# The shared expert's last gate and up quarter, moved ahead of the first pair's row picking

## The reference, cut to what matters

```
scores = sigmoid(xf @ router_w)                     # 256 tokens x 64 experts
idx    = top_k(scores + router_b, 6)
wts    = sel / sum(sel) * 2.5
routed = sum over a token's 6 experts of ((silu(x @ w_gate[e]) * (x @ w_up[e])) @ w_down[e]) * weight
shared = (silu(xf @ sh_gate) * (xf @ sh_up)) @ sh_down
x = x + g2 * (routed + shared)
```

## Time and profile before

| what | us |
|---|---|
| median of 3 runs | 1473.63 |
| lowest and highest of them | 1473.15, 1475.94 |
| the profiled execution's own time | 1474.18 |
| its span, first to last instruction | 1472.3 |
| PE busy | 1311.8 (89%) |
| DVE busy | 631.6 (43%) |
| ACT busy | 296.9 (20%) |
| HBM read | 496.57 MB, 340 GB/s over the span |

### The profile page before, as it was taken

The page is one execution under the profiler, slowest core; times in us unless marked ns, Lnnn a source line. Parts: engine busy times, 40 slices in busy tenths (PEclk is TensorE's granted clock), DMA queues, the critical chain, the costliest instruction groups (busy, mean ns, idle before and its releaser), DMA issues.

```text
span 1472.3 us, 21785 instructions
## 1 busy us (share of the span) xinstructions
PE 1311.8 (89%) x9040; PEld 684.9 (47%) x9040; DVE 631.6 (43%) x1165; ACT 296.9 (20%) x504; POOL 66.7 (5%) x116
## 2 busy tenths in 40 slices
PE   4998868999999879888898999989999978888888
PEld 1444325764444334344346766875444433333334
DVE  5997733254433222232234688654443222232232
ACT  3236322321111111111112113031111111111110
POOL 0000681000000000000000000000000000000000
PEclk9999889999999999999997999999999999999999
DMA  9672972958999999999999772575899999999996
GB/s 379 251 179 75 175 283 92 397 226 341 400 422 421 429 423 428 428 430 426 429 419 324 289 256 94 233 323 223 355 422 421 425 428 428 428 430 427 427 426 246
DMA packets 50583, 502.78 MB, mean 341 GB/s; under 512 B 9324, under 2 KB 16236, under 8 KB 19820
## 3 DMA queue, kind: packets, MB, share of 16 engines
q1 hardware_dynamic: 49932, 499.18, 85.1%
q10 hardware_dynamic: 544, 2.10, 0.3%
HBM read 496.57 MB, written 4.69 MB: 340 GB/s over the span
## 4 chain that ended last, share of the span: by engine, by line
PE 59%; DMA 32%; DVE 4%; issue 2%; ACT 1%; SPq 1%; DVEq 0%; ACTq 0%
PE ps L704 54%; DMA arena<-in_w_experts 28%; DMA arena<-in_ada_w 4%; PE ps L428 2%; PE ps L1011 2%; SPq L472 1%; ACT arena L1323 1%; DVE arena L1941 1%; PE ps L749 0%; DMA arena<-in_mcst 0%; DVE arena L1775 0%; DVE arena L1776 0%; PE ps L957 0%; DVE arena L1793 0%; DVE arena L1773 0%
## 5 line engine op out<-in xcount | busy, mean ns | idle before, releaser
L704 PE MATMUL ps<-arena 128*32 128x512 f32 (+13 forms) x8220 | 1227.0, 487 | 138.5 <-issue 52.3
L704 PEld LDWEIGHTS ps<-arena 128*32 128x32 f32 (+6 forms) x8220 | 622.9, 131 | 728.8 <-issue 589.7
L1323 ACT ACTIVATE arena<-ps 128x512 f32<-128x512 f32 (+7 forms) x304 | 168.0, 553 | 943.2 <-PE ps L704 799.2
L1982 DVE SCALAR_TENSOR_TENSOR arena<-arena,ps 128x256 f32<-128x256 f32 x44 | 21.2, 481 | 242.1 <-ACT arena L1323 242.1
L1323 ACT ACTIVATE arena<-arena 128x256 f32<-128x256 f32 (+7 forms) x140 | 91.6, 680 | 162.8 <-DVE arena L2002 58.6
L2000 DVE CAST arena<-ps 128x512 bf16<-128x512 f32 x42 | 29.1, 692 | 164.9 <-PE ps L704 164.9
L1937 DVE COPY arena<-ps 128x512 f32<-128x512 f32 x44 | 30.4, 692 | 135.5 <-PE ps L704 135.5
L1970 DVE TENSOR_TENSOR arena<-arena 128x1024 bf16<-128x1024 f32 x42 | 51.5, 1225 | 37.3 <-ACT arena L1323 37.0
L694 POOL MEMSET arena<- 128x1 f32 x2 | 0.2, 102 | 1206.1 <-PE ps L1011 1206.1
L1011 PE MATMUL ps<-arena 128*128 128x128 f32 x352 | 52.8, 273 | 0.0
L2002 DVE TENSOR_TENSOR arena<-ps,arena 128x1024 f32<-128x1024 f32 x42 | 51.4, 1224 | 1.8 <-DVE arena L2000 0.4
(11 more groups left out here) (226 smaller groups left out, 475.3 us busy)
## 6 DMA issues: line engine op xcount, KB each, us to landing
arena<-in_w_experts SPq DMA_DIRECT2D x76, 3072.0 KB, 20.8
arena<-in_w_experts SPq DMA_DIRECT2D x52, 2048.0 KB, 19.5
arena<-in_w_experts SPq DMA_DIRECT2D x52, 1024.0 KB, 18.9
arena<-in_ada_w SPq DMA_DIRECT2D x40, 1024.0 KB, 6.1
arena<-in_hy_w_in SPq DMA_DIRECT2D x6, 2048.0 KB, 11.2
arena<-in_ada_w SPq DMA_DIRECT2D x4, 2048.0 KB, 22.3
arena<-in_w_shared SPq DMA_DIRECT2D x2, 3072.0 KB, 10.5
arena<-in_hy_w_out SPq DMA_DIRECT2D x1, 4096.0 KB, 13.3
```

What stands on the lines that cost most here:

```text
L704: return pe.matmul(out, lhsT, rhs, start=start, stop=stop, skip_group_check=skip)
L1323: return act.activation(out, in_, func, **kw)
L1982: stt(hh, sg, wtab[:, n:n + 1], ps[:, GU, FF:2 * FF], M, M).then_inc(sem("h_done"), 1)
```

## The change

One line moves. The fourth quarter of the shared expert's gate and up product, with its `sh_gu`, is issued right behind the third one and ahead of `pick_rows(0)`, where it was behind `turn_rows(0)`.

```diff
                 mm(ps[0:1, 0, 3 * NE:4 * NE], extent, ident[:, 0:NE], True, True).then_inc(sem("route_mm"), 1)
                 shared_gate_up(2)
+                shared_gate_up(3).then_inc(sem("sh_gu"), 1)
                 pick_rows(0)
                 find_tokens(0)
                 turn_rows(0)
-                shared_gate_up(3).then_inc(sem("sh_gu"), 1)
```

## The result

The changed kernel is slower by a little. Its median is 1478.13 us (20 runs, 1471.74 to 1481.46) against 1474.10 us for the kernel before in the same comparison, a ratio of 1.0022 with a 95% interval of 1.0011 to 1.0032. That is +3.2 us (+1.6 to +4.7); the two medians themselves differ by 4.0. Forecast were 1475.4 us, or +1.76, which lies in the lower part of that interval.

A forecast was written before the change was run, and what follows sets the result against it. PE was taken to bound each layer's expert part until the loads' stage starts at 370, the loads after that. A new wait of 0.88 us per layer, 1.76 in all, on 1473.63 gave 1475.4 us, 8 in 10 within 1473.0 to 1478.5.

The forecast's parts named there:

- The bound: Each layer's expert part: PE's progress up to 370 sets when the loads begin, so its lost time reaches the layer's end.
- loads' stage: Second stage of each layer's expert part, from the triple issued at 370.0: loads run without a gap, at 422 GB/s.
- The quarter covers the copy: Behind the turning the quarter hid DVE's copy of the turned rows; moving it bares a wait, taken as 0.88 us per layer.
- The cover ahead of the picking is empty: Ahead of the picking PE never waited, so the quarter covers nothing there and picking and turning start 3.40 us later.
- The queues: Behind the turning: DVE's shared expert product starts near 324.5 with 4 us left; SP's earlier load gains nothing.
- load at place 5: SP's 2 MB load that waits for the quarter: issued 5.7 us earlier, near 315.8, worth nothing at 370.
- The clock: Around group 0's gate and up product: granted clock expected to stay up despite PE's pauses of 0.69 and 0.86 us.
- The whole: Whole kernel: 1475.4 us, which is 1473.63 + 1.76, or 0.12%; chance of the same within 0.2%: 0.80.
- +0.88 in layer 0, +0.88 again: Sum over both layers' expert parts: one new wait each, passed on undiminished, 1.76 us in all.
- forecast's own 1474 to 1477.5: Whole kernel: range with scatter of medians if only a wait of 0.7 to 1.2 us per layer is added; 76 in 100.
- 1473.0 to 1478.5 of 8 in 10: Whole kernel: wider range, reaching to the case of no move and to most of the falling clock's case.
- the clock's rival: Group 0's gate and up product: clock falls to 1.2 GHz, 2.57 us per layer with the wait, 1478.8; 9 in 100.

The follow-up runs named there:

- split kernels: Kernel before with the fourth quarter halved around the turning, in one version also two steps of quarter 1 moved ahead of the routing wait: ratios 0.9999, 0.9995, 0.9995.
- e4: Kernel before with the fourth quarter moved whole between the table look-up and the turning: ratio 1.0003 (0.9988 to 1.0018).
- f4: Kernel before with the third quarter too moved behind the turning, ahead of the fourth: ratio 1.0050 (1.0034 to 1.0067).
- f2: Kernel before with DVE's copy of the first pair's turned rows made four times per layer instead of once: ratio 1.0004 (0.9991 to 1.0017).
- f3: Changed kernel with DVE's copy of the first pair's turned rows made four times per layer: ratio 1.0081 (1.0055 to 1.0108).
- f1: Changed kernel, with the first half of the load at place 5 waiting for group 0's gate and up product: ratio 1.0023 (1.0008 to 1.0039).
- g1: Kernel before, unaltered, compared with itself as if it were a changed one: ratio 1.0006 (0.9992 to 1.0020).
- e1: Changed kernel run again with no edit, against the kernel before: ratio 1.0024 (1.0008 to 1.0040).
- split quarter: Kernel before with the fourth quarter halved, one half ahead of the turning, one behind it: ratios 0.9999 and 0.9995 in two comparisons.
- g2: Changed kernel a third time, no edit, on the same chip as the unaltered kernel before: ratio 1.0047 (1.0029 to 1.0065).

## Why the prediction was right, and where it was short

**The bound.** Right. PE sets the start of the loads' stage, and the distance shifts as PE does; the stage behind it gives nothing back. Between the triple's issue and the first load for the next layer's mixer lie 397.35 us before and 397.17 after, and from layer 1's triple to the first store of the output 412.69 and 412.76. (In layer 0 the split kernels have 397.8 to 398.3, but so have e4 and f4 with 397.8 and 397.9, so this is not laid to the split.)

**The quarter covers the copy.** Right, and shown by f2 and f3. Forecast 0.88 per layer, measured 0.95 and 0.94: 0.86 to 0.88 of it is the pause, and nearly all of the rest is that the quarter takes 3.46 us ahead of the picking and had filled 3.40 behind the turning. The prediction took 3.40 for both.

**The cover ahead of the picking is empty.** Right: nothing is gained there.

**The queues.** Right. DVE's product began 2.5 us behind the copy's end (325.02 to 327.57), with 4 us to spare. The load at place 5 was 5.5 us early, forecast 5.7, and f1 shows it to be worth nothing.

**The clock.** Right that it stays. The two pauses of 0.69 and 0.87 us left it at 1.00 within the distance, in both layers of all four profiles of the changed kernel (f1's among them). The grounds were too narrow: the prediction weighed one fall, behind a pause of over 4 us, and left out those at shorter pauses in the same trace, such as the one at 0.62 us ahead of layer 0's routing, so its 9 in 100 rest on less than was there. Of the rule that it cites from the Trainium skill (TensorE: Matmul & The Clock Gate, "A second HAM failure mode: psum-queue depth-cycling"), that brief idling between groups of matmuls makes the clock swing, the runs show this much: two brief pauses close together did not make the clock swing here, and one of 3.05 us was followed by a fall.

**The whole.** Short. The three comparisons of the changed kernel (42 runs) have a mean of 1477.7 us, and the kernel before beside them (82 runs) 1473.8: +3.9 us, with a standard error of 0.5, where the distances give 1.9. The step that fell short is the last one, "+0.88 in layer 0, +0.88 again" and nothing else: some 2 us of the whole do not come from there. It also put the chance of a change within 0.2% at 0.80, and 1.0022 lies just beyond that. The 1478.13 us are outside the forecast's own 1474 to 1477.5 and inside the 1473.0 to 1478.5 of 8 in 10, by 0.4 us; that upper end was set for the clock's rival, which did not come true, so this is in part luck.

Where are those 2 us? Not in the loads' stages, which last alike, and not in the stretch up to layer 0's routing, which lies ahead of the change: it is 297.8 us before, 300.8, 298.0 and 299.2 in three profiles of the changed kernel, 298.1 and 304.7 in g1 and f2. The mixer of layer 1 with what lies around it is left (213.4 before; 212.5, 208.5, 212.6; 209.7 in both g1 and f2). It scatters by more than what is sought, and it scatters with the clock. In the 14 profiles it lasts from 208.5 us at a granted clock of 0.96 (e1) to 214.2 at 0.93 (e4), and the stretch ahead of layer 0's routing from 295.6 at 0.94 (f3) to 304.7 at 0.89 (f2), though no kernel differs from another there.

So the runs have to be compared at equal clock too. Each run has a mean granted clock, and within each of three kernels (before, changed, split quarter) the time falls as it rises, by 5 to 6.5 us for 0.01. Over all their runs the kernel before (99) has 0.9599 and the changed one (42) 0.9578. At a clock of 0.960 a straight line through each gives 1473.6 and 1476.3, a difference of 2.7 us (standard error 0.3); with f1's runs counted as the changed kernel's it is 2.7 again. For the split quarter (24 runs, clock 0.9576) it is 1472.2, or -1.4 where its distance says -1.6. This comparison was thought of after the runs, but it is the best sign that the distance reaches the whole. Of the 3.9 us, then, 1.9 are the distances', about 1.2 go with a lower clock somewhere outside them, and 0.8 are in neither.

Nor is the rest peculiar to this change. All thirteen ratios of the table lie above the one that their distance gives, from 0.0001 (e4) and 0.0006 (g1, the kernel before against itself) to 0.0026 (f4) and 0.0034 (g2). They share their runs of the kernel before, so they are not thirteen witnesses. Whether the comparison leans, or shifting the later work against the clock costs, or the sample of runs does this, is not settled; f2, which has the distance of before, also has a clock of 0.9580.

## What to carry to other kernels

Work that fills a wait belongs behind the instruction whose result must be copied out, not ahead of one that never waited: count for each wait what stands between producer and consumer, and cut the filler so that each wait gets as much as it is long (the split quarter did this: 0.82 us less per layer in the distance). A transfer that is started earlier gained nothing here, since the next ones wait for something that is not earlier. Where the whole scatters by more than the effect, read a distance inside the trace that encloses the change, and then still check the whole, at equal clock as well, since the two did not agree fully here.

## What the runs showed of the hardware

- The handover from PE to a copy of 128x512 float32 on DVE and back to PE took 0.86 to 0.88 us here, of which the copy is 0.69.
- The granted clock stayed at its upper level with pauses of 0.69 and 0.87 us close together (all profiles of the changed kernel), and fell to the lower one for some us behind a pause of 3.05 us (f3, in both layers), which cost 1.7 and 2.9 us on top. But a fall followed only 9 of 21 equal pauses of 2.11 us (kernel before), and it also fell with no pause at all, while PE was busy with 128x1 products (e4, at 288.8): the length of a pause alone does not tell.
- A stretch of unchanged work took 208.5 us at a granted clock of 0.96 and 214.2 at 0.93 (layer 1's mixer, e1 and e4). Most of the scatter of the whole lies in this stretch and in the one ahead of layer 0's routing.
- The distance read here, in which the clock stayed at 1.00, repeats within 0.03 us over separate executions and chips, while the whole scatters by some 10 us.
